# Alternating the high and low matmuls of the chunks with stationary weights in a float32 transformer block

## The chip, the cores and the metric

The kernel runs on one core of one Trainium2 chip, in one launch. The metric is the device time of the whole program in microseconds. Before the change it is 1725.64 us, the median of three runs (1724.52 to 1726.35).

## The reference

One layer of a hybrid streaming encoder, for 256 rows of 2048 columns, all in float32:

```
h = rmsnorm(x, g_mix);  z = h @ w_in            # 2048 x 14848
o_a = hgrn2_mixer(...)                           # gated linear recurrence, 16 heads
o_b = swa_sink_attention(...)                    # banded attention, 32 heads
x = x + concat(sigmoid(gate_a)*o_a, sigmoid(gate_b)*o_b) @ w_out      # 4096 x 2048
h = rmsnorm(x, g_mlp)
x = x + square(relu(h @ w_up)) @ w_down          # 2048 x 8192, 8192 x 2048
x = x + sigmoid(x @ w_ple_gate) * (p @ w_ple_proj)
return rmsnorm(x, g_final)
```

The change lies in `h @ w_up` alone, and there in seven eighths of its columns.

## The kernel before, in words

**Products in three parts.** Every large product is made of float32 operands that are split into a high part, rounded to the type that TensorE multiplies at one pass (`F32R` in the code), and a low part, the rounding's remainder. Of the four products of parts the kernel keeps three: high by high, low activations by high weights, and high activations by low weights. The activations lie transposed in SBUF as `hT` (128 partitions, 16 slices of the contraction, high or low, 2 row tiles, 128 rows); `hT_hi` and `hT_lo` are its halves.

**Chunks.** The weights stream through SBUF in 588 chunks of 256 rows by 512 columns (two slices `kk` of 128 rows). SyncE loads a chunk into one of 4 slots of `w_raw`. ScalarE rounds it into `w_hi` (`split_hi`, L980), once the slot's former user has been read (`w_used` of four chunks earlier). VectorE subtracts and writes `w_lo` (`split_lo`, L1337); that also frees the slot of `w_raw`. TensorE works the chunks in order; `w_hi_ready` and `w_lo_ready` count the chunks split, and the last matmul of a chunk raises `w_used`. ScalarE and VectorE run ahead of TensorE and do the work between the products (`steps`, `mlp_steps`) in between, in an order written out by hand, three chunks behind the splits (`LAG`).

**Two shapes of chunk.** In most chunks the activations are the stationary operand (128 by 128) and the weights move, 512 columns at a time: twelve matmuls a chunk, at L679 (high activations), L680 (low activations) and L685 (low weights). In the chunks of `up` with `j > 0` it is turned around (`turned_chunk`): the weights are stationary, 128 columns of them at a time (`ct` 0 to 3), and the activations move. With `w_hi` stationary all 512 columns of `hT` move, high and low, 2 row tiles (L693). With `w_lo` stationary the 256 columns of `hT_hi` move (L699), and are added to the first half of the same PSUM bank. The result comes out transposed, as `down` needs it. Each `ct` has its own bank (`turned_acc`): two banks named `acc` and two named `turn`. So a turned chunk is 8 matmuls of 512 columns and 8 of 256, each with its own weight load of 128 by 128.

**Order and loops.** The up and down products come in groups of 1024 hidden columns. Two blocks `up` (8 chunks each) are followed by the four blocks `down` of the group before (16 chunks in all). `up` with `j = 1` stands before the loop; a hardware loop of 3 rounds does two groups a round, and what is left of `down` follows it. That makes 14 turned blocks, and behind each pair of them a stretch of 16 `down` chunks: seven pairs, seven stretches.

**The wait.** Before its first matmul a chunk waits for `w_hi_ready` (in `chunk`, L669). A turned chunk then issues its 8 matmuls on `w_hi`, waits for `w_lo_ready`, and issues its 8 on `w_lo`. The first chunk of a block has further waits, for PSUM banks that must be empty (`free_before`).

Of the kernel before, what the change touches and what calls it, by code (L numbers as in the profile page):

```python
# [34 lines left out]
P = 128  # L35
TT = 2
# [97 lines left out]
def program(nc, x, p, positions, g_mix, w_in, lb_logits, hgrn_norm_g, sinks, w_out,  # L134
            g_mlp, w_up, w_down, w_ple_gate, w_ple_proj, g_final, out):
    with ExitStack() as ctx:
        def sb(name, shape, dt=F32):
            return ctx.enter_context(nc.sbuf_tensor(name, shape, dt))
# [3 lines left out]
        hT = sb("hT", [P, KT, 2, TT, P], F32R)  # L142
        hT_hi, hT_lo = hT[:, :, 0], hT[:, :, 1]
        w_raw = sb("w_raw", [P, RAW_SLOTS, 2, COLS])
        w_hi = sb("w_hi", [P, W_SLOTS, 2, COLS], F32R)
        w_lo = sb("w_lo", [P, W_SLOTS, 2, COLS], F32R)
# [182 lines left out]
        def count(value, r=0, per=0):  # L329

            return value + r * per
# [71 lines left out]
        def turned_acc(col, ct):  # L403

            return (acc[(UP_BANKS + col) % 2] if ct < 2 else T[2 * col:2 * col + 2])[ct % 2]
# [52 lines left out]
        def bank(name):  # L458
            return T[uses[name][0]]
# [183 lines left out]
        def _(pe):  # L643
# [9 lines left out]
            def chunk(slot, r=0):  # L653
# [16 lines left out]
                if turned(kind, j):  # L670
                    turned_chunk(n, col, c, s, first, last, r)
                    return
# [15 lines left out]

            def turned_chunk(n, col, c, s, first, last, r):

                for kk in range(2):
                    for ct in range(4):
                        pe.matmul(turned_acc(col, ct)[:], w_hi[:, s, kk, ct * P:(ct + 1) * P],  # L693
                                  hT[:, 2 * c + kk].rearrange("p a t c -> p (a t c)"),
                                  start=first and kk == 0, stop=False)
                pe.wait_ge(w_lo_ready, count(n + 1, r, LOOP_CHUNKS))
                for kk in range(2):
                    for ct in range(4):
                        mm = pe.matmul(turned_acc(col, ct)[:, 0:TT * P], w_lo[:, s, kk, ct * P:(ct + 1) * P],  # L699
                                       hT_hi[:, 2 * c + kk].rearrange("p t c -> p (t c)"), start=False,  # L700
                                       stop=last and kk == 1)
                mm.then_inc(w_used, 1)
# [225 lines left out]
            for slot in TAIL:  # L928
# [7 lines left out]
                if n == DOWN7:  # L936
                    pe.wait_ge(p_landed, 16)
                    for t in range(TT):
# [3 lines left out]
                        for k in range(2):  # L942
                            mm = pe.transpose(bank(name)[:, k * P:(k + 1) * P],
                                              pe_sb[:, t, k * P:(k + 1) * P], ident[:])
# [877 lines left out]
```

## Time and profile before

| what | value |
|---|---|
| median of three runs | 1725.64 us |
| span of the profiled execution, first to last instruction | 1722.8 us |
| TensorE matmuls busy | 1700.2 us, 99% of the span, 8685 instructions |
| TensorE weight loads busy | 1416.5 us, 82% |
| VectorE busy | 1105.8 us, 64% |
| ScalarE busy | 925.0 us, 54% |
| mean granted TensorE clock | 0.998 |

The profile gives the profiled execution its span and no other time of its own. The median of the runs lies 2.8 us above that span. "Busy" is the share of the span in which at least one instruction of the engine is recorded. Matmuls overlap in the records, so the duration of one says less than the distance from its start to the next one's start; below that distance is called a step. PE is TensorE's matmuls, PEld its weight loads, DVE VectorE, ACT ScalarE, and a q behind a name is the engine's sequencer.

### The profile page before, as it was taken

Reading aid. Unit: us, or ns where it says so; the run is one execution under the profiler, and the core shown is the slowest. Engines: PE = TensorE matmul, PEld = TensorE weight load, DVE = VectorE, ACT = ScalarE, POOL = GpSimd, SP = SyncE. Lnnn points to the kernel's source line nnn. Section 1 sums busy time; section 2 is a strip of 40 time slices with the busy share of each in tenths; the row PEclk is TensorE's granted clock in tenths of the full one; section 3 lists DMA queues with packets and bytes.
Section 4 is the critical chain, followed back from the end, with each engine's and each line's share of the span. In section 5 each row is a group of like instructions: output and inputs, shape, how many; then the busy total and the mean of one; then the engine's idle time right before and its main releaser. Section 6 shows DMA issues by size and latency. Waiting matters only on the chain.

```text
span 1722.8 us, 23521 instructions
## 1 busy us (share of the span) xinstructions
PE 1700.2 (99%) x8685; PEld 1416.5 (82%) x8685; DVE 1105.8 (64%) x1409; ACT 925.0 (54%) x1227; POOL 18.2 (1%) x72
## 2 busy tenths in 40 slices
PE   7999999999999999999999999999999999999997
PEld 6887887788887888878888888888888888888886
DVE  6667866875668756687585555656555556566565
ACT  6566646555566555655546554544444445454454
POOL 4000000000000000000000000000000000000000
PEclk9999999999999999999999999999999999999999
DMA  6665555556655566555556666666666666666554
GB/s 221 203 176 172 172 177 164 172 179 176 184 180 171 175 180 186 172 173 178 176 178 212 184 191 188 194 189 193 189 192 188 193 185 191 190 191 186 182 181 138
DMA packets 163293, 315.35 MB, mean 183 GB/s; under 512 B 10161, under 2 KB 10482, under 8 KB 163058
## 3 DMA queue, kind: packets, MB, share of 16 engines
q1 hardware_dynamic: 162016, 312.01, 59.8%
q10 hardware_dynamic: 1170, 1.87, 0.3%
q8 instruction: 73, 1.20, 0.3%
q14 instruction: 34, 0.28, 0.0%
HBM read 311.74 MB, written 2.10 MB: 182 GB/s over the span
## 4 chain that ended last, share of the span: by engine, by line
PE 96%; ACT 2%; DVE 1%; DMA 0%; issue 0%; SPq 0%; ACTq 0%; DVEq 0%
PE acc L679 21%; PE acc L680 21%; PE acc L685 21%; PE acc L693 6%; PE turn L693 6%; PE turn L685 3%; PE turn L680 3%; PE turn L679 3%; PE turn L699 3%; PE acc L699 3%; PE turn L721 2%; ACT w_hi L980 0%; PE turn L772 0%; ACT pr L1033 0%; PE turn L748 0%; PE turn L819 0%
## 5 line engine op out<-in xcount | busy, mean ns | idle before, releaser
L1337 DVE TENSOR_TENSOR w_lo<-w_raw,w_hi 128x1024 fp32r<-128x1024 f32 x588 | 720.0, 1224 | 564.5 <-ACT w_hi L980 561.6
L980 ACT ACTIVATE w_hi<-w_raw 128x1024 fp32r<-128x1024 f32 x588 | 622.7, 1059 | 709.9 <-PE acc L685 452.9
L679 PE MATMUL acc<-w_hi,hT 128*128 128x512 f32 x1104 | 436.0, 395 | 4.2 <-DVE hT L1377 4.2
L680 PE MATMUL acc<-w_hi,hT 128*128 128x512 f32 x1104 | 430.9, 390 | 0.0
L685 PE MATMUL acc<-w_lo,hT 128*128 128x512 f32 x1104 | 295.4, 389 | 0.0
L679 PEld LDWEIGHTS acc<-w_hi,hT 128*128 128x128 f32 x1104 | 207.9, 188 | 48.1 <-ACT w_hi L980 5.3
L685 PEld LDWEIGHTS acc<-w_lo,hT 128*128 128x128 f32 x1104 | 207.3, 188 | 43.5
L680 PEld LDWEIGHTS acc<-w_hi,hT 128*128 128x128 f32 x1104 | 208.0, 188 | 41.6
L679 PE MATMUL acc<-w_hi,mT_hi 128*128 128x512 f32 x416 | 164.5, 395 | 0.0
L680 PE MATMUL acc<-w_hi,mT_lo 128*128 128x512 f32 x416 | 162.3, 390 | 0.0
L693 PE MATMUL acc<-hT,w_hi 128*128 128x512 f32 x448 | 140.2, 394 | 0.6 <-issue 0.5
L693 PE MATMUL turn<-hT,w_hi 128*128 128x512 f32 x448 | 138.8, 391 | 0.0
L685 PE MATMUL acc<-w_lo,mT_hi 128*128 128x512 f32 x416 | 111.4, 390 | 0.0
L693 PEld LDWEIGHTS turn<-hT,w_hi 128*128 128x128 f32 x448 | 84.1, 188 | 19.2
L679 PEld LDWEIGHTS acc<-w_hi,mT_hi 128*128 128x128 f32 x416 | 78.1, 188 | 18.0 <-ACT w_hi L980 2.4
L685 PEld LDWEIGHTS acc<-w_lo,mT_hi 128*128 128x128 f32 x416 | 78.1, 188 | 16.5
L680 PEld LDWEIGHTS acc<-w_hi,mT_lo 128*128 128x128 f32 x416 | 78.2, 188 | 15.6
L699 PE MATMUL turn<-hT,w_lo 128*128 128x256 f32 x448 | 90.3, 283 | 0.0
L699 PE MATMUL acc<-hT,w_lo 128*128 128x256 f32 x448 | 89.5, 282 | 0.0
L693 PEld LDWEIGHTS acc<-hT,w_hi 128*128 128x128 f32 x448 | 77.3, 190 | 11.4 <-issue 1.5
L699 PEld LDWEIGHTS acc<-hT,w_lo 128*128 128x128 f32 x448 | 77.0, 190 | 8.7
L699 PEld LDWEIGHTS turn<-hT,w_lo 128*128 128x128 f32 x448 | 69.5, 191 | 0.0
(250 smaller groups left out, 1554.9 us busy)
## 6 DMA issues: line engine op xcount, KB each, us to landing
w_raw<-in_w_in_dram SPq DMA_DIRECT2D x232, 512.0 KB, 3.7
w_raw<-in_w_up_dram SPq DMA_DIRECT2D x128, 512.0 KB, 3.7
w_raw<-in_w_down_dram SPq DMA_DIRECT2D x128, 512.0 KB, 4.6
w_raw<-in_w_out_dram SPq DMA_DIRECT2D x64, 512.0 KB, 3.8
w_raw<-in_w_ple_gate_dram SPq DMA_DIRECT2D x32, 512.0 KB, 4.5
x_sb<-in_x_dram SPq DMA_DIRECT2D x8, 256.0 KB, 7.8
w_raw<-in_w_ple_proj_dram SPq DMA_DIRECT2D x4, 512.0 KB, 4.4
out_dram<-x_sb SPq DMA_DIRECT2D x6, 256.0 KB, 3.0
```

The costliest lines, as they stand in the source:

```text
L679: pe.matmul(a, hi[:, k, t, :], w_hi[:, s, kk, :], start=first and kk == 0, stop=False)
L680: pe.matmul(a, lo[:, k, t, :], w_hi[:, s, kk, :], start=False, stop=False)
L685: mm = pe.matmul(acc_of(kind, j, col, t)[:], hi[:, k, t, :], w_lo[:, s, kk, :], start=False, stop=last and kk == 1)
L693: pe.matmul(turned_acc(col, ct)[:], w_hi[:, s, kk, ct * P:(ct + 1) * P], hT[:, 2 * c + kk].rearrange("p a t c -> p (a t c)"), start=first ...
L699: mm = pe.matmul(turned_acc(col, ct)[:, 0:TT * P], w_lo[:, s, kk, ct * P:(ct + 1) * P], hT_hi[:, 2 * c + kk].rearrange("p t c -> p (t c)") ...
L721: mm = pe.transpose(bank(name)[:, i * P:(i + 1) * P], src(i), ident[:])
L980: act.activation(w_hi[:, n % W_SLOTS], w_raw[:, n % RAW_SLOTS], ACT.Copy)\
L1337: dve.tensor_tensor(w_lo[:, n % W_SLOTS], w_raw[:, n % RAW_SLOTS], w_hi[:, n % W_SLOTS].bitcast(F32), ALU.subtract).then_inc(w_lo_ready, 1)
```

## The change

In a turned chunk the eight matmuls on `w_hi` no longer come first and the eight on `w_lo` last. For each `kk` and `ct` the matmul of 512 columns on `w_hi` is issued, and right behind it the one of 256 columns on `w_lo`, into the same bank. The wait for `w_lo_ready` therefore stands ahead of the chunk's first matmul, beside the one for `w_hi_ready`. The number, shapes and operands of matmuls and weight loads stay the same, and so do all signals.

```diff
             def turned_chunk(n, col, c, s, first, last, r):
 
-                for kk in range(2):
-                    for ct in range(4):
-                        pe.matmul(turned_acc(col, ct)[:], w_hi[:, s, kk, ct * P:(ct + 1) * P],
-                                  hT[:, 2 * c + kk].rearrange("p a t c -> p (a t c)"),
-                                  start=first and kk == 0, stop=False)
                 pe.wait_ge(w_lo_ready, count(n + 1, r, LOOP_CHUNKS))
                 for kk in range(2):
                     for ct in range(4):
-                        mm = pe.matmul(turned_acc(col, ct)[:, 0:TT * P], w_lo[:, s, kk, ct * P:(ct + 1) * P],
+                        cs = slice(ct * P, (ct + 1) * P)
+                        pe.matmul(turned_acc(col, ct)[:], w_hi[:, s, kk, cs],
+                                  hT[:, 2 * c + kk].rearrange("p a t c -> p (a t c)"),
+                                  start=first and kk == 0, stop=False)
+                        mm = pe.matmul(turned_acc(col, ct)[:, 0:TT * P], w_lo[:, s, kk, cs],
                                        hT_hi[:, 2 * c + kk].rearrange("p t c -> p (t c)"), start=False,
                                        stop=last and kk == 1)
                 mm.then_inc(w_used, 1)
```

## Rows read from the trace of the kernel before

**Rows 1.** Page, parts 1 and 2: busy time, share, instructions; TensorE's clock in tenths.

```profile
PE 1700.2 (99%) x8685; PEld 1416.5 (82%) x8685; DVE 1105.8 (64%) x1409; ACT 925.0 (54%) x1227; POOL 18.2 (1%) x72
...
PEclk9999999999999999999999999999999999999999
```

**Rows 2.** Page, part 4: the chain that ended last, by engine.

```profile
PE 96%; ACT 2%; DVE 1%; DMA 0%; issue 0%; SPq 0%; ACTq 0%; DVEq 0%
```

**Rows 3.** Waits: who waited for whom, us in total, times, longest.

```profile
ACT w_hi L980 <- PE turn L699: 158.3, 104, 2.5
...
PEld acc L679 <- ACT w_hi L980: 7.8, 5, 4.5
```

**Rows 4.** Page, part 5: TensorE's groups in turned chunks; count, busy, mean ns.

```profile
L693 PE MATMUL acc<-hT,w_hi 128*128 128x512 f32 x448 | 140.2, 394 | 0.6 <-issue 0.5
L693 PE MATMUL turn<-hT,w_hi 128*128 128x512 f32 x448 | 138.8, 391 | 0.0
```

**Rows 5.** Timeline of PE, first two turned chunks: start us, us, instruction, count.

```profile
945.37 0.62 PE L693 MATMUL acc<-hT,w_hi 128*128 128x512 f32 x2
...
947.19 0.40 PE L699 MATMUL acc<-hT,w_lo 128*128 128x256 f32 x2
947.42 0.40 PE L699 MATMUL turn<-hT,w_lo 128*128 128x256 f32 x2
...
947.90 0.40 PE L699 MATMUL turn<-hT,w_lo 128*128 128x256 f32 x2
948.14 0.63 PE L693 MATMUL acc<-hT,w_hi 128*128 128x512 f32 x2
948.61 0.62 PE L693 MATMUL turn<-hT,w_hi 128*128 128x512 f32 x2
...
949.98 0.40 PE L699 MATMUL acc<-hT,w_lo 128*128 128x256 f32 x2
...
950.93 0.63 PE L693 MATMUL acc<-hT,w_hi 128*128 128x512 f32 x2
```

**Rows 6.** Durations ns (min/median/max) of L699, 947.1 to 948.2 us.

```profile
L699 PE MATMUL acc<-hT,w_lo x4: 278/282/283, 947.2 to 947.8; 128*128 128x256 f32 x4
```

**Rows 7.** Timeline of PE L685, four matmuls a row, in two stretches of `down`.

```profile
1346.81 1.08 PE L685 MATMUL acc<-w_lo,aT_hi 128*128 128x512 f32 x4
...
1360.54 1.08 PE L685 MATMUL turn<-w_lo,aT_hi 128*128 128x512 f32 x4
1436.23 1.07 PE L685 MATMUL acc<-w_lo,mT_hi 128*128 128x512 f32 x4
...
1449.83 1.07 PE L685 MATMUL turn<-w_lo,mT_hi 128*128 128x512 f32 x4
```

**Rows 8.** Windows of L685 in `down` stretches: us, PE busy, PEld busy, clock, DMA.

```profile
996.90:1029.60 32.70, 12.97 (x48) 9.02 (x48) 1.00 0.63 196
1086.70:1119.40 32.70, 12.83 (x48) 9.07 (x49) 1.00 0.63 194
```

**Rows 9.** Timeline of all engines behind a turned chunk: matmuls and their next loads.

```profile
1079.55 0.40 PE L679 MATMUL acc<-w_hi,mT_hi 128*128 128x512 f32 x1
1079.55 0.19 PEld L680 LDWEIGHTS acc<-w_hi,mT_lo 128*128 128x128 f32 x1
1079.78 0.40 PE L680 MATMUL acc<-w_hi,mT_lo 128*128 128x512 f32 x1
```

**Rows 10.** Timelines of DVE, ACT and PE before the turned chunk of 1076.75 us.

```profile
1070.49 1.22 DVE L1337 TENSOR_TENSOR w_lo<-w_raw,w_hi 128x1024 fp32r<-128x1024 f32 x1 [0.26 <-ACT w_hi L980]
...
1071.42 1.06 ACT L980 ACTIVATE w_hi<-w_raw 128x1024 fp32r<-128x1024 f32 x1 [0.96 <-PE turn L699]
...
1076.75 0.63 PE L693 MATMUL acc<-hT,w_hi 128*128 128x512 f32 x2
```

**Rows 11.** TensorE's sequencer at L669: its separate waits, ns min/median/max.

```profile
L669 PEldq EVENT_SEMAPHORE x73: 51/51/2467, 57.0 to 1686.4; - x73
```

## The prediction

> **What bounds the kernel now.** I read the page's busy shares first, and there the reader sees TensorE's matmuls busy for 99% of the span at the upper of its two clock levels (nines in every slice, so 2.4 GHz) [rows 1]. Then the chain of waits: 96% of it is TensorE [rows 2]. Then the waits: TensorE hardly waits for the split weights (7.8 us in the whole run, all in chunks of the other shape), while ScalarE waits 104 times for the end of a turned chunk [rows 3]. So the splits run ahead, and only what shortens or lengthens TensorE's own steps can move the time. Last the timeline, for the length of a step, which is where this change acts.
>
> **How long a chunk takes.** L693 has 448 + 448 matmuls, eight a chunk, so 112 turned chunks [rows 4]. The second one runs from 948.14 to 950.93, which is 2.79 us: its eight steps of 512 columns take 949.98 - 948.14 = 1.84 us and its eight of 256 take 0.95 us [rows 5]. (Of another chunk the rows give 2.80, 1076.75 to 1079.55 [rows 9, 10]. I take 2.795.) Together the turned chunks are 112 x 2.795 = 313 us.
>
> Four kinds of step can be told apart:
> - 512 columns in a steady run of them: 13.60 us for 60 matmuls (1436.23 to 1449.83, five chunks of twelve), so 0.2267 us [rows 7].
> - 256 columns in a steady run: two in 0.24 us, so 0.120 [rows 5].
> - 256 columns right after a run of 512: the first two take 0.23 us together [rows 5], and the shortest duration of the eight is 278 ns where the usual is 283 [rows 6]. The first is thus some 5 to 7 ns short, about 0.113.
> - 512 columns right after the run of 256: two in 0.47 us (948.14 to 948.61), so 0.235 each, where the first turned chunk, which came from a run of 512, takes (947.19 - 945.37) / 8 = 0.2275 on average [rows 5]. The whole excess is 1.84 - 1.82 = 0.02 us a chunk.
>
> The first two steps differ by 0.2267 - 0.120 = 0.1067 us for 256 columns, 0.417 ns a column, one column at 2.4 GHz. Take the columns off either and the same 13.3 ns remain (0.2267 - 0.2133; 0.120 - 0.1067). So both steady runs cost columns plus a fixed 13.3 ns for each pair of load and matmul, whatever the length. I take that as the law, and two things as disturbances of a change between runs: 7 ns saved once, some 27 ns paid afterwards.
>
> **The change part by part.**
>
> *The order.* Nothing is added or removed: 8 long and 8 short steps a chunk before and after. By the law a pair is 0.2267 + 0.120 = 0.3467 us and the chunk 8 x 0.3467 = 2.773, against 2.795 now. That is 0.022 us a chunk, 112 x 0.022 = 2.4 us less. The trace shows no single short step between long ones. Its bounds by the nearest rows: a pair of at least 0.2267 + 0.113 = 0.340, if every short step is like the first of its run; at most 0.235 + 0.120 = 0.355, if every long step is like those right behind a run of 256. I take the law, since it fits both steady runs without a free constant, and an alternation that repeats is a steady run too; it lies between the bounds.
>
> *The weight load.* A load starts with the matmul ahead of its own (the load for L680 at 1079.55, with the matmul of L679, and L680's own at 1079.78) [rows 9]. So one load is in flight beside one matmul, and no order of matmuls lets loads run further ahead. Under a short matmul now lies the load of a long one's weights. It is the same 128 by 128, and short steps follow each other at 0.120 with it. No cost.
>
> *The same bank twice in a row.* The short matmul now adds to the bank that the long one ahead of it writes. L679 and L680 do that in each chunk of the other shape, at a step of 0.23 (1079.55 to 1079.78) [rows 9], like all steps there. No cost.
>
> *The earlier wait.* `w_lo_ready` is asked for at the chunk's start and no longer 1.84 us into it. Queued behind it are all matmuls of the chunk, and behind their end ScalarE's next split. For the chunk at 1076.75 the split is long done. ScalarE's split at 1071.42 was released by the end of a turned chunk, the fourth ahead of its own. That one ended 2 x 2.79 us before 1076.75, so the split is for the chunk after the one at 1076.75, and the latter's `w_lo` is the one from 1070.49, ended at 1071.71 [rows 10]. That leaves 5.0 us of cover. It is at the end of a pair of blocks, behind the extra work on activations, where the cover should be thinnest. Cost nothing; if the cover were gone, the wait would expose up to 1.84 us a chunk. The instruction itself is one more on the sequencer, 51 ns each [rows 11]. The 73 such waits that L669 already has leave no trace in the chain, where issue has 0% [rows 2], so I count nothing. If none were hidden it would be 112 x 0.051 = 5.7 us.
>
> *What is left behind.* In the `down` stretches behind the turned pairs steps come in two steady patterns. From 1346.81 to 1360.54 they are 13.73 / 60 = 0.2288, from 1436.23 to 1449.83 0.2267, for the same shapes [rows 7]. Of the seven stretches four show the first kind (12.97 us for 48 matmuls of L685) and three the second (12.83), of each kind one is shown [rows 8]. The slow kind costs 27 ns a chunk, 4 x 16 x 0.027 = 1.7 us over the run. Which kind a stretch takes seems to hang on how it is entered, and the change alters that for all seven. All fast would save 1.7 us, all slow cost 3 x 16 x 0.027 = 1.3 us. I can't tell which, and take zero.
>
> *The sum* is 1722.8 - 2.4 = 1720.4 us of span. The median lies 2.8 us over the span before, so 1723.2 us. A difference of 0.2% (3.45 us) is about what a measurement of this kernel can tell from none.
>
> **The rivals.**
> - *The short step is free of the extra.* Every short matmul behind a long one steps at 0.113, as the first of a run does in the trace. A pair is 0.340, a chunk 2.72, 112 x 0.075 = 8.4 us less: 1717.2 us. For it: the first short step is short in [rows 5, 6]. Against it: what that one saves is followed by long steps that pay more than it, so it may be lent and not given. Chance 0.20.
> - *The long step never settles.* Behind a short step each long one costs 0.235, and the short ones stay at 0.120. A pair is 0.355, a chunk 2.84, 112 x 0.045 = 5.0 us more: 1730.6 us, slower. For it: those are the two steps that the trace shows at that very change [rows 5], and now there are eight such changes a chunk instead of one. Against it: they come behind eight short matmuls, where loads had followed each other closely; one short matmul may leave no such trail. It decides from a pair of 0.3494 on (2.795 / 8), above which the order loses. Chance 0.16.
> - *The order doesn't matter.* Steps neither gain nor lose, or settle into a pattern like the slow one of `down` (0.2288 + 0.120 = 0.3488, a chunk of 2.79): 1725.1 to 1725.6 us. Chance 0.14. The Trainium skill (TensorE: Matmul & The Clock Gate, Step-by-step: what each phase is for) comes to the same by another road: it says that weights are read through a port of their own and that loading the next ones takes nothing from the running matmul. By it both orders would be exactly equal, and the time 1725.6. The constant 13.3 ns in both kinds of step [rows 5, 7] doesn't decide whether it is the load's doing; that the runs of short steps disturb the long ones behind them speaks against full independence.
> - *The earlier wait is exposed.* VectorE's split comes late for some chunks. With 5.0 us of cover [rows 10] it would take a delay of two chunks. If the first chunk of each of the 14 blocks lost 1.84 us it would be 25.8 us more, 1751 us. Chance 0.02. The wait's instruction unhidden (+5.7 us, 1728.9 with the forecast's gain) gets 0.02.
>
> **How the numbers follow.** The forecast has 0.46: 1723.2 us, its own range 1721.3 to 1724.8 with what the `down` stretches may add. Of it 0.06 lies beyond 0.2% faster (if those stretches also turn fast, 4.1 us less in all). Faster: 0.20 + 0.06 = 0.26, and I say 0.28, as some pairs may lie between 0.340 and 0.347. Slower: 0.16 + 0.02 + 0.02 = 0.20. The same: 0.52. The range reaches down over the free short step (1717.0) and up to 1729.5, which leaves out the full price of the step that never settles and the exposed wait.
>
> **What would show it.** In the timeline of a turned chunk the rows alternate L693 and L699; the distance from one L693 to the next is the pair: 0.347 by the forecast, 0.340, 0.355 and 0.349 by the rivals. The chunk is 2.77, 2.72, 2.84 or 2.79. The first short step of a pair sits 0.227 behind its long one. The waits list no wait of L693 for `w_lo`; if it does, the cover was misread. The windows of L685 in the seven `down` stretches show 12.97 or 12.83 us, and the difference to the four and three of before is to be booked apart from the change itself. The prediction is wrong if a pair lies outside 0.343 to 0.351, or if the time moves by more than 3.45 us.

## The result, and the profile after

The changed kernel takes 1728.11 us (median of 20 runs, 1725.96 to 1729.89), against 1724.89 us for the kernel before in the same runs (1724.05 to 1726.35). The ratio is 1.0017, 95% interval 1.0012 to 1.0023: 3.2 us slower, where 2.4 us less were forecast. The interval lies clear of 1, though the difference is only 0.2%. The profiled execution took 1728.99 us, 1.7 us more than its span.

From the page after, the span, the busy shares, the chain by engine, and the two groups of the turned chunks on `acc` (line, engine, operation, count, busy us, mean ns, idle before):

```profile
span 1727.3 us, 23633 instructions
...
PE 1704.1 (99%) x8685; PEld 1415.9 (82%) x8685; DVE 1105.4 (64%) x1409; ACT 924.8 (54%) x1227; POOL 16.6 (1%) x72
...
PE 97%; ACT 1%; DVE 1%; DMA 0%; issue 0%; SPq 0%; ACTq 0%; DVEq 0%
...
L695 PE MATMUL acc<-hT,w_hi 128*128 128x512 f32 x448 | 168.3, 398 | 1.3 <-issue 1.3
...
L698 PE MATMUL acc<-hT,w_lo 128*128 128x256 f32 x448 | 125.8, 281 | 0.0
```

TensorE has as many matmuls as before and bounds the kernel as before [rows 1, 2]. The long matmuls are longer, 398 ns on average where 394 stood [rows 4]. No wait for `w_lo` is behind it. The only wait of a matmul in these chunks is this one (who waited for what: us in total, times, longest; "issue" is idle time in which the engine waited for nothing that the profile shows):

```profile
PE acc L695 <- issue: 1.3, 2, 0.8
```

The timeline tells more. First a chunk of the third turned block, the first of the loop (start us, us, instruction, count):

```profile
1038.24 0.40 PE L695 MATMUL acc<-hT,w_hi 128*128 128x512 f32 x1
1038.48 0.28 PE L698 MATMUL acc<-hT,w_lo 128*128 128x256 f32 x1
...
1039.30 0.40 PE L695 MATMUL turn<-hT,w_hi 128*128 128x512 f32 x1
...
1041.07 0.40 PE L695 MATMUL acc<-hT,w_hi 128*128 128x512 f32 x1
```

Then one of the second turned block:

```profile
969.29 0.39 PE L695 MATMUL acc<-hT,w_hi 128*128 128x512 f32 x1
969.52 0.28 PE L698 MATMUL acc<-hT,w_lo 128*128 128x256 f32 x1
...
970.33 0.39 PE L695 MATMUL turn<-hT,w_hi 128*128 128x512 f32 x1
...
972.07 0.39 PE L695 MATMUL acc<-hT,w_hi 128*128 128x512 f32 x1
```

Three pairs take 1.06 us in the first and 1.04 in the second; chunks take 2.83 and 2.78 (2.827 and 2.773 on average over a block, from the starts that the trace holds to the ns). So there are two steady paces. The fast one is the forecast's, 0.3467 us a pair: 230 + 117 ns. The slow one repeats after three pairs, 233 + 117, 241 + 120, 236 + 113 ns, 0.3533 on average. Which one a block runs in can be read from windows of 17 us over the L695 instructions (window, its length, PE busy, PEld busy, clock, DMA): the faster a block goes, the more of its weight loads fall in the window.

```profile
972.30:989.30 17.00, 17.00 (x50) 9.18 (x50) 1.00 0.62 182
1038.40:1055.40 17.00, 17.00 (x49) 9.02 (x48) 1.00 0.63 187
```

All twelve blocks of the loop show 9.02 to 9.05, the slow pattern; only the blocks before the loop turn fast, and they do so behind the eight transposes that stand after their third chunk:

```profile
954.55 1.03 PE L720 MATMUL turn<-ident,u_sb 128*128 128x128 f32 x8
...
956.47 0.39 PE L695 MATMUL turn<-hT,w_hi 128*128 128x512 f32 x1
...
956.81 0.39 PE L695 MATMUL acc<-hT,w_hi 128*128 128x512 f32 x1
```

The account: 12 chunks at 2.773 and 100 at about 2.827 are 315.9 us, where 112 at 2.793 were 312.8. That is 3.1 us of the 3.2 us by which the medians differ. Added up from the starts of the two traces, the turned chunks take 316.1 and 313.0 us.

The spans of the two profiled executions lie further apart than that, 1727.3 and 1722.8. Of these 4.5 us, 3.0 are in the turned chunks. Another 0.7 lies ahead of the first turned chunk, which starts at 946.08 where it started at 945.37 [rows 5], although the two kernels are the same up to there, and 0.8 lies between the turned blocks, outside the steps of `down`. In the other runs whose kernel is the same up to there, the first turned chunk starts anywhere from 944.9 to 947.4 us. So one span tells little at this size, and the steps inside the chunks tell more.

The `down` stretches did not change. Two rows 5 chunks apart of a stretch on aT, and two of one on mT:

```profile
998.81 1.07 PE L685 MATMUL acc<-w_lo,aT_hi 128*128 128x512 f32 x4
...
1012.54 1.07 PE L685 MATMUL turn<-w_lo,aT_hi 128*128 128x512 f32 x4
1261.15 1.07 PE L685 MATMUL acc<-w_lo,mT_hi 128*128 128x512 f32 x4
...
1274.75 1.07 PE L685 MATMUL turn<-w_lo,mT_hi 128*128 128x512 f32 x4
```

13.73 and 13.60 us again [rows 7], and again four stretches of the first kind and three of the second.

### The profile page after: what moved, and what is told of

Read it like the earlier page. It is cut to its first block, busy times and chain, and to the rows that moved or that the text cites. A ratio compares the mean times of both kernels' runs of the same rounds, so it can differ in the third digit from the quotient of the medians.

```text
span 1727.3 us, 23633 instructions
## 1 busy us (share of the span) xinstructions
PE 1704.1 (99%) x8685; PEld 1415.9 (82%) x8685; DVE 1105.4 (64%) x1409; ACT 924.8 (54%) x1227; POOL 16.6 (1%) x72
## 3 DMA queue, kind: packets, MB, share of 16 engines
q10 hardware_dynamic: 1170, 1.87, 0.3%
## 4 chain that ended last, share of the span: by engine, by line
PE 97%; ACT 1%; DVE 1%; DMA 0%; issue 0%; SPq 0%; ACTq 0%; DVEq 0%
PE acc L679 22%; PE acc L680 21%; PE acc L685 21%; PE acc L695 6%; PE turn L695 6%; PE turn L679 3%; PE turn L685 3%; PE turn L680 3%; PE acc L698 3%; PE turn L698 3%; PE turn L720 2%; PE turn L747 0%; PE turn L771 0%; PE turn L818 0%; PE turn L759 0%; DMA w_raw<-in_w_in_dram 0%
## 5 line engine op out<-in xcount | busy, mean ns | idle before, releaser
L685 PE MATMUL acc<-w_lo,hT 128*128 128x512 f32 x1104 | 296.0, 390 | 0.0
L685 PEld LDWEIGHTS acc<-w_lo,hT 128*128 128x128 f32 x1104 | 207.8, 188 | 43.7
L695 PE MATMUL acc<-hT,w_hi 128*128 128x512 f32 x448 | 168.3, 398 | 1.3 <-issue 1.3
L695 PE MATMUL turn<-hT,w_hi 128*128 128x512 f32 x448 | 168.1, 398 | 0.0
L698 PE MATMUL acc<-hT,w_lo 128*128 128x256 f32 x448 | 125.8, 281 | 0.0
L698 PE MATMUL turn<-hT,w_lo 128*128 128x256 f32 x448 | 125.8, 281 | 0.0
L685 PE MATMUL acc<-w_lo,mT_hi 128*128 128x512 f32 x416 | 111.5, 390 | 0.0
L695 PEld LDWEIGHTS acc<-hT,w_hi 128*128 128x128 f32 x448 | 84.1, 188 | 22.6 <-issue 2.1
L695 PEld LDWEIGHTS turn<-hT,w_hi 128*128 128x128 f32 x448 | 84.1, 188 | 20.8
L685 PEld LDWEIGHTS acc<-w_lo,mT_hi 128*128 128x128 f32 x416 | 78.1, 188 | 16.6
L698 PEld LDWEIGHTS acc<-hT,w_lo 128*128 128x128 f32 x448 | 84.6, 189 | 0.2
L698 PEld LDWEIGHTS turn<-hT,w_lo 128*128 128x128 f32 x448 | 84.6, 189 | 0.0
```

The costliest lines, as they stand in the source:

```text
L685: mm = pe.matmul(acc_of(kind, j, col, t)[:], hi[:, k, t, :], w_lo[:, s, kk, :], start=False, stop=last and kk == 1)
L695: pe.matmul(turned_acc(col, ct)[:], w_hi[:, s, kk, cs], hT[:, 2 * c + kk].rearrange("p a t c -> p (a t c)"), start=first and kk == 0, stop ...
```

## The experiments

All change `turned_chunk` or the place of buffers. The diffs are cut to the lines that matter. Where the order changes, the rest is the changed kernel with its early wait; where only a buffer moves, the rest is the kernel before unless the text says otherwise. A run marked "one execution" was timed once: its steps, which repeat from chunk to chunk, are read, and its time is only given beside them. `grouped(g)` below stands for the order: g long matmuls, then their g short ones, until the chunk's eight pairs are done. `grouped(8)` is the order before, `grouped(1)` the changed one.

**The wait alone.** The order before, with the wait at the chunk's start.

```diff
+                pe.wait_ge(w_lo_ready, count(n + 1, r, LOOP_CHUNKS))
                 for kk in range(2):
                     for ct in range(4):
                         pe.matmul(turned_acc(col, ct)[:], w_hi[:, s, kk, ct * P:(ct + 1) * P],
 ...
-                pe.wait_ge(w_lo_ready, count(n + 1, r, LOOP_CHUNKS))
```

> The order of before (eight long matmuls, then eight short), with only the wait for the low part moved to the chunk's start. Theory (two steady patterns of the alternating stream, 0.3467 and 0.3533 us a pair, the second being the price): the wait costs nothing, a turned chunk stays at 2.79 us and the time is that of before. Rival (the earlier wait or its instruction costs): a chunk of 2.82 us and 3 us more than before.

Measured: 1725.40 us, ratio 1.0005 (0.9995 to 1.0014). A block of it runs from chunk to chunk as before:

```profile
1058.12 0.63 PE L695 MATMUL acc<-hT,w_hi 128*128 128x512 f32 x2
...
1063.71 0.63 PE L695 MATMUL acc<-hT,w_hi 128*128 128x512 f32 x2
```

Two chunks in 5.59 us, and all turned chunks together 313.0 us, as in the trace before. The earlier wait and its instruction cost nothing that the trace shows; the order carries the cost.

**Two by two.**

```diff
-                for kk in range(2):
-                    for ct in range(4):
+                for what, kk, ct in grouped(2):
```

> Two long matmuls, then their two short ones, four times a chunk, so that no matmul adds to the bank of the one ahead of it. Rival (writing one bank twice in a row costs 6.7 ns a pair): the cost is gone, the chunk is 2.77 us and the time some 2.4 us under before. Theory (steady patterns that depend on how a stretch is entered): again one or two steady patterns with a mean pair between 0.3467 and 0.3533, chunk 2.77 to 2.83, whatever the bank; 0.3467 is the floor.

Measured: 1724.71 us, ratio 1.0000 (0.9990 to 1.0009). The chunk is 2.787 us in one pattern throughout, here 1062.52 to 1065.31:

```profile
1062.52 0.63 PE L695 MATMUL acc<-hT,w_hi 128*128 128x512 f32 x2
...
1065.31 0.62 PE L695 MATMUL acc<-hT,w_hi 128*128 128x512 f32 x2
```

With the double write to one bank gone the chunk is still not 2.77, so the rival of the bank is not borne out, though this run changes the order too. The run with equal lengths below settles it, and so do the alternating blocks that run at 2.773 us with every bank written twice in a row.

**Four by four.**

```diff
-                for kk in range(2):
-                    for ct in range(4):
+                for what, kk, ct in grouped(4):
```

> Four long matmuls, then their four short ones, twice a chunk. Theory: chunk 2.77 to 2.83, no step pattern under 0.3467 a pair on average. Rival (each change from short to long costs a fixed sum, 20 ns a chunk for one change before): two changes cost 40 ns, chunk 2.81 us, and two-by-two would be 2.85 us.

Measured: 1727.03 us, ratio 1.0014 (1.0004 to 1.0023), chunk 2.807 us. By itself it would fit a fixed price per change of length, 14 ns for the second. But four changes (two by two) cost 6 ns less than one, and eight cost 34 more or 20 less. No fixed price per change fits.

**Other entries.** The first chunk of a block in another order, the rest alternating.

```diff
+                if c:
+                    return grouped(1)
+                if n < HEAD_CHUNKS:
+                    return grouped(8)
+                second = n - HEAD_CHUNKS >= LOOP_CHUNKS // 2
+                if second:
+                    return grouped(8) if col else grouped(4)[:8] + grouped(1)[8:]
+                return grouped(2) if col else grouped(8)
```

> Alternating as in the changed kernel, but the first chunk of a block is ordered otherwise: eight by eight in both blocks before the loop and in the first and last block of a loop round, two by two in the second, four by four for its first slice in the third. Theory: the chunks behind settle in 2.774 us (0.3467 a pair) or 2.827 us (0.3533), the same one in all three rounds for the same entry, and at least one of the entries reaches the fast pattern, as the burst of transposes in the first turned block did in the changed kernel. Rival (the slow pattern belongs to the loop's code, say to its register waits, and the fast one to the chunks before the loop): all chunks in the loop stay at 2.827 us whatever the entry.

Measured (one execution, 1727.40 us): the second block of each loop round, entered two by two, is fast in all three rounds (9.19 or 9.20 us in its window); the other three are slow. Eight by eight threw the second block before the loop out of the fast pattern that the first had ended in. Windows over L695 of that second block, and of the first two of a round:

```profile
972.10:989.10 17.00, 17.00 (x49) 9.02 (x48) 1.00 0.60 180
1038.70:1055.70 17.00, 17.00 (x49) 9.06 (x49) 1.00 0.65 187
1061.30:1078.30 17.00, 17.00 (x50) 9.20 (x50) 1.00 0.61 182
```

The entry changes the pace, and the loop's code can run either.

**More entries**, of the same kind.

```diff
+                if n < HEAD_CHUNKS:
+                    return grouped(2)
+                second = n - HEAD_CHUNKS >= LOOP_CHUNKS // 2
+                if second:
+                    return grouped(1) if col else grouped(3)[:6] + grouped(1)[6:]
+                return grouped(2) if col else grouped(2)[:4] + grouped(1)[4:]
```

> Alternating, with other entries: both blocks before the loop start with a chunk two by two; in a loop round the first block starts with one group of two by two and then alternates, the second with a whole chunk two by two, the third with two groups of three, the fourth as in the changed kernel. Theory: each entry leads to one of the two patterns, the same in all three rounds, and the fourth block goes on in the pattern of the third. Rival (chance, or drift within a block): the pattern differs between rounds or changes inside a block without a disturbance.

Measured (one execution, 1727.32 us): the same entry gave different paces. The first block of a round turned fast in round one and slow in the two others, where a loop jump lies ahead of it. The second, two by two, turned slow where it came from fast and fast where it came from slow. Yet the second block before the loop, also two by two, came from fast and stayed fast. The first two blocks of rounds one and two:

```profile
1038.10:1055.10 17.00, 17.00 (x50) 9.16 (x49) 1.00 0.63 187
1060.30:1077.30 17.00, 17.00 (x49) 9.02 (x48) 1.00 0.59 179
...
1216.30:1233.30 17.00, 17.00 (x49) 9.02 (x49) 1.00 0.63 186
1239.00:1256.00 17.00, 17.00 (x50) 9.19 (x49) 1.00 0.58 182
```

My expectation that an entry decides by itself failed. The starts to the ns show what was different: the fast pace has two patterns. One is 230 + 117 ns in every pair; the block that turned slow had come from it. The other is 233 + 117 and 231 + 113 in turn, with the same mean of 0.3467; the block that stayed fast had come from that one. So the pace goes with the entry together with the pattern that the stream comes in. Inside a block the pace never changed without a disturbance.

**Two by two at the entry of each pair of blocks.**

```diff
+                return grouped(2) if c == 0 and col == 0 else grouped(1)
```

> The changed kernel, but the first chunk of each of the seven pairs of blocks goes two by two (two long, their two short), all others alternate. Two by two led the second block of a loop round into the fast pattern three times of three. Theory (two steady patterns, chosen by the entry): all chunks behind the first take 2.773 us, the turned chunks 310.7 us in all, 2.3 us less than before and 5.3 less than the changed kernel, so about 1722.5 us. Rival (what counts is the state in which the block before ended, and two by two helps only behind the slow pattern): behind a down stretch the chunks stay at 2.827 us and the time is that of the changed kernel, 1728 us.

Measured: in the trace all chunks behind the entries are fast, with 9.19 or 9.20 us in 13 windows and the 14th holding the transposes, all in the pattern 233 + 117, 231 + 113 ns; the turned chunks sum to 310.9 us, and the span is 1721.6. The time without a profile is 1724.47 us, ratio 1.0000 (0.9991 to 1.0009), where 1722.5 was expected. The interval still holds 0.9991, that is 1.6 us less. The profiled execution, 1723.34 us, is the shortest of the eleven, which go up to 1726.88. Whether the unprofiled runs took the fast pattern everywhere can't be seen, so this run shows that the fast pace can be had in every block and leaves its worth open.

**Short matmuls of 384 columns.**

```diff
-                        mm = pe.matmul(turned_acc(col, ct)[:, 0:TT * P], w_lo[:, s, kk, cs],
-                                       hT_hi[:, 2 * c + kk].rearrange("p t c -> p (t c)"), start=False,
+                        mm = pe.matmul(turned_acc(col, ct)[:, 0:3 * P], w_lo[:, s, kk, cs],
+                                       hT[:, 2 * c + kk].rearrange("p a t c -> p (a t c)")[:, 0:3 * P],
```

> The changed kernel with short matmuls of 384 columns instead of 256 (they add a fourth product of parts for one row tile, so more is computed than wanted). Theory (a pair of load and matmul costs its columns plus 13.3 ns; the slow pattern arises because a load just fits into the short step): 0.2267 + 0.1733 = 0.400 us a pair in all blocks, a chunk of 3.20 us, and only one pattern. Rival (any change of length disturbs the steps): again two patterns, or steps of the long ones of 0.233 to 0.241, and a chunk of 3.25 us in the loop.

Measured (one execution, 1779.37 us): two paces again, 0.4133 us a pair (chunk 3.307) and 0.4067 (chunk 3.253), neither of them 0.400. From a slow block and from a fast one, eight pairs each:

```profile
1072.56 0.40 PE L695 MATMUL acc<-hT,w_hi 128*128 128x512 f32 x1
...
1075.86 0.40 PE L695 MATMUL acc<-hT,w_hi 128*128 128x512 f32 x1
1142.51 0.39 PE L695 MATMUL acc<-hT,w_hi 128*128 128x512 f32 x1
...
1145.76 0.39 PE L695 MATMUL acc<-hT,w_hi 128*128 128x512 f32 x1
```

Six of the fourteen blocks are fast and eight slow, and here the transposes in the first block end the fast pace instead of starting it. My explanation, that the load only just fits under a step of 256 columns, is wrong: with some 55 ns more room (a short step of 175 ns) the slow chunk lies 107 ns over the law's, where it lay 54 over. The law is not kept here even at the faster pace. No run has 384 columns alone, so its term for them, 0.1733, is itself untested.

**Both matmuls of 512 columns.**

```diff
-                        mm = pe.matmul(turned_acc(col, ct)[:, 0:TT * P], w_lo[:, s, kk, cs],
-                                       hT_hi[:, 2 * c + kk].rearrange("p t c -> p (t c)"), start=False,
+                        mm = pe.matmul(turned_acc(col, ct)[:], w_lo[:, s, kk, cs],
+                                       hT[:, 2 * c + kk].rearrange("p a t c -> p (a t c)"),
```

> The changed kernel with both matmuls of a pair 512 columns long (the second adds the product of the low parts, which is more than wanted). Theory now (it is the alternation of lengths that disturbs, not the alternation of w_hi and w_lo as loads and not the same bank twice): all steps 0.2267 us, a chunk of 3.627 us, in one pattern. Rival (same bank or alternating sources of the load): steps over 0.2267, a chunk of 3.68 us or more, or two patterns.

Measured (one execution, 1819.29 us): 227 ns a step, 3.627 us a chunk, in all blocks; here one of sixteen steps, 3.63 us:

```profile
1049.32 0.39 PE L695 MATMUL acc<-hT,w_hi 128*128 128x512 f32 x1
...
1052.95 0.39 PE L695 MATMUL acc<-hT,w_hi 128*128 128x512 f32 x1
```

Same bank twice, `w_hi` and `w_lo` loaded in turn, 16 loads a chunk: all free here. What costs is that the lengths change. This run has no short step, so it says nothing on a load under one.

**The address of aT.** Of the kernel before, with 64 bytes of padding ahead of `u_sb`.

```diff
+            lb_("pad", [P, 16])
             u_sb = lb_("u_sb", [P, 2, TT, COLS])
```

> The kernel of before with 64 bytes of padding a partition ahead of u_sb, so that aT_hi, aT_lo, pT_hi and pT_lo begin at a multiple of 128 bytes, as mT and hT do; nothing else. It is on the step of 0.2288 us in four down stretches (those whose stationary operand is aT). Theory: the address of the stationary operand sets it, and all seven stretches show 0.2267 (12.83 us in the windows), some 1.8 us less. Rival (the prediction's: how a stretch is entered decides): nothing changes, four stretches stay at 12.97 us.

Measured: 1723.29 us, ratio 0.9990 (0.9981 to 0.9999), 1.6 us less. All seven stretches are of the fast kind. A stretch on aT, five chunks:

```profile
1355.21 1.07 PE L686 MATMUL acc<-w_lo,aT_hi 128*128 128x512 f32 x4
...
1368.81 1.07 PE L686 MATMUL acc<-w_lo,aT_hi 128*128 128x512 f32 x4
```

13.60 us, where such a stretch took 13.73 [rows 7]. The four stretches save 0.4 us each in the trace, which is the 1.6 us. The address decides, and not the entry, as I had put it.

**The mirror.** The padding ahead of `mT_hi` instead.

```diff
+        sb("pad", [P, 16])
         mT_hi = sb("mT_hi", [P, 8, TT, P], F32R)
```

> The kernel of before with the 64 bytes of padding ahead of mT_hi instead, so that mT begins 64 bytes past a multiple of 128 and aT, behind it, at a multiple. Theory (a stationary operand 64 bytes off a multiple of 128 costs 2.3 ns a step): now the stretches on aT run at 0.2267 us and the three on mT at 0.2288, and so do the output projection's chunks on mT. Rival (something else of aT, or the padding's other effects): the four or none of them are slow.

Measured (one execution): 1731.02 us. Five chunks on aT take 13.60, five on mT 14.00:

```profile
1360.54 1.07 PE L686 MATMUL acc<-w_lo,aT_hi 128*128 128x512 f32 x4
...
1374.14 1.07 PE L686 MATMUL acc<-w_lo,aT_hi 128*128 128x512 f32 x4
1443.71 1.10 PE L686 MATMUL acc<-w_lo,mT_hi 128*128 128x512 f32 x4
...
1457.71 1.10 PE L686 MATMUL turn<-w_lo,mT_hi 128*128 128x512 f32 x4
```

The direction is as expected. The size is not: 0.2333 us a step, 6.7 ns over the fast one and not 2.3.

**The weights moved 64 bytes.** Order as before.

```diff
+        sb("pad", [P, 16])
         w_hi = sb("w_hi", [P, W_SLOTS, 2, COLS], F32R)
         w_lo = sb("w_lo", [P, W_SLOTS, 2, COLS], F32R)
+        sb("pad2", [P, 16])
```

> The kernel of before with w_hi and w_lo moved 64 bytes off a multiple of 128 (padding ahead of w_hi and behind w_lo; mT stays at a multiple, aT at 64 past one). In the turned chunks they are the stationary operand, in all others the moving one. Theory (the address of what is loaded counts, since the load's reading gets in the way of the running matmul's): the turned chunks take more than 2.793 us, and the down stretches on mT keep their 0.2267 us a step. Rival (any operand's address counts, the moving one's too): the down stretches on mT and the chunks on hT slow down as well, and the whole kernel by 10 us or more.

Measured (one execution): 1736.52 us, against 1725.16 for the kernel before beside it. The theory fails. Of the rival, the slower mT and hT and the 10 us or more come out, but not its rule that any operand off its place costs: aT and the turned chunks get faster. Five chunks on aT, four on mT, and five on hT:

```profile
1179.04 1.07 PE L687 MATMUL acc<-w_lo,aT_hi 128*128 128x512 f32 x4
...
1192.64 1.07 PE L687 MATMUL turn<-w_lo,aT_hi 128*128 128x512 f32 x4
1445.85 1.10 PE L687 MATMUL acc<-w_lo,mT_hi 128*128 128x512 f32 x4
...
1457.05 1.10 PE L687 MATMUL turn<-w_lo,mT_hi 128*128 128x512 f32 x4
421.32 1.08 PE L687 MATMUL acc<-w_lo,hT 128*128 128x512 f32 x4
...
435.06 1.08 PE L687 MATMUL acc<-w_lo,hT 128*128 128x512 f32 x4
```

aT, off by 64 bytes like the weights, is now fast (13.60 for five chunks); mT, moved by 128 bytes in all, and hT, not moved, are slow (11.20 for four, 13.74 for five). It is the distance between the loaded and the moving operand that counts. The turned chunks got faster, 2.773 us in nearly all, in the order of before:

```profile
1051.95 0.62 PE L695 MATMUL acc<-hT,w_hi 128*128 128x512 f32 x2
...
1053.82 0.39 PE L701 MATMUL acc<-hT,w_lo 128*128 128x256 f32 x2
...
1054.05 0.39 PE L701 MATMUL turn<-hT,w_lo 128*128 128x256 f32 x2
...
1054.73 0.62 PE L695 MATMUL acc<-hT,w_hi 128*128 128x512 f32 x2
```

But not their long steps: eight long ones take 1.87 us here and took 1.84 [rows 5], the eight short ones 0.91 and took 0.95. The last six short steps take 0.68 us, 113.3 ns each, where a run of them stepped at 120; the long ones end up between 231 and 236, 233.3 on average over two. The two sum to 346.7 ns, as 226.7 and 120 do at the old distance. The moved weights shift time from the short step to the long one, and the chunk gains because the change of length costs less.

**The alternation with the weights moved so.** The same two lines of padding in the changed kernel.

> The changed kernel (alternating) with w_hi and w_lo 64 bytes off a multiple of 128, as in the run before, so that in the turned chunks the loaded and the moving operand no longer have the same remainder by 128 bytes. In the order of before that took the turned chunk from 2.793 to 2.773 us. Theory (the extra over columns plus 13.3 ns comes from the addresses at which load and stream read at once): the slow pattern is gone and all turned chunks take 2.773 us whatever the entry. Rival (the alternation of lengths makes the slow pattern by itself, whatever the addresses): most blocks of the loop stay at 2.827 us.

Measured (one execution): 1741.02 us; one pattern, 235 + 118 ns, 2.827 us a chunk in every block, also behind the transposes:

```profile
1046.15 0.40 PE L697 MATMUL acc<-hT,w_hi 128*128 128x512 f32 x1
...
1048.98 0.40 PE L697 MATMUL acc<-hT,w_hi 128*128 128x512 f32 x1
```

The theory falls. At this distance grouping by eight gives 2.773 and alternating 2.827, whatever the entry. So the slow pace comes with the alternation at both distances tried, and the fast one was seen only where loaded and moving operand have the distance that they have in the changed kernel. The long step, 235 ns, is much like the 233.3 of the grouped order at this distance; the short one is 118 and not 113.

**The weights moved 128 bytes**, order as before.

```diff
+        sb("pad", [P, 32])
         w_hi = sb("w_hi", [P, W_SLOTS, 2, COLS], F32R)
```

> A control: the kernel of before with 128 bytes of padding ahead of w_hi, so that everything behind moves but no remainder by 128 changes. Theory (only the remainder by 128 bytes counts): the trace of before again, turned chunks of 2.793 us, down stretches on aT at 0.2288 and on mT at 0.2267 us a step. Rival (any move of the weights against the activations shifts the patterns): other values.

Measured (one execution): 1745.33 us, against 1723.98 beside it. The control fails and with it the remainder by 128. Five chunks on hT take 13.95 us:

```profile
420.18 1.09 PE L686 MATMUL acc<-w_lo,hT 128*128 128x512 f32 x4
...
434.13 1.09 PE L686 MATMUL acc<-w_lo,hT 128*128 128x512 f32 x4
```

In the `down` stretches on aT and mT, whose distance from the weights did not change, it left the steps at 0.229 and 0.227 us.

Sorted by the distance modulo 256 bytes (address of the loaded operand less that of the moving one, addresses from the compiled program), all runs agree. By 512 bytes the remainders 192 (aT before) and 448 (hT with w +64) gave the same step, and so did 0 and 256, which is why the remainder is taken by 256. Steps are the trace's means in us. In the middle column the weights move; turned chunks load w and move hT:

```
distance   step of 512 columns in a run             turned chunk, grouped(8) / grouped(1)
0          0.2267 (hT, mT before; aT with padding)   2.793 / 2.827 or 2.773
64         0.2333 (mT in the mirror and with w +64)  2.773 / 2.827
128        0.2325 (hT with w +128)                   2.799 and 2.821 in turn / not run
192        0.2289 (aT before; hT with w +64)         not run
```

**Entry and padding together.**

```diff
+            lb_("pad", [P, 16])
             u_sb = lb_("u_sb", [P, 2, TT, COLS])
 ...
+                return grouped(2) if c == 0 and col == 0 else grouped(1)
```

> The alternating order entered two by two, and the 64 bytes of padding that align aT. Theory: the down stretches run at 0.2267 us a step (1.7 us less than before), the chunks behind each entry at 2.773 us (2.1 us less in all), since both kinds of stretch ahead of a block are now alike: about 3.9 us under before, 1721 us. Rival (the pattern of the trace is not what the runs without a profile do, as the kernel entered two by two was only 0.5 us under before): 1.7 us under before, no more, as with the padding alone.

Measured: 1722.23 us against 1725.42 for the kernel before on the same chip, ratio 0.9983 (0.9974 to 0.9992), 3.2 us less. The whole interval lies below the kernel before. The trace has all `down` stretches and all turned chunks behind their entries fast, and a span of 1719.7 us. 1.6 us of the gain is the padding's by the run above. The rest, some 1.6 us of the expected 2.1, would be the alternation's, but the intervals of this run and of the padding alone overlap, so that part is not shown by the times.

## Why the prediction was wrong

**The step that failed is the law taken for the alternation**: "an alternation that repeats is a steady run too", so 0.3467 us a pair. It is one of two paces at which the stream settles, and TensorE took the other, 0.3533, in all twelve blocks of the loop. The term *The order* was to be -0.022 us a chunk, 2.4 us less, and is +0.027 on average, 3.0 us more. The deciding point, 0.3494 a pair, lies between the two. The rival that never settles had the right sign, and nearly the size (0.355 against 0.3533). It had the mechanism half: long steps of 233 to 241 ns, as behind a run of short ones, but short steps of 113 to 120 and not all of 120. That the size is so near is partly luck: the long steps average 236.7 where it had 235, the short ones 116.7 where it had 120. I had given it 0.16 because a single short matmul "may leave no such trail"; it does.

**The sign of it could have been seen in the rows.** The long steps behind the short run (0.235) were the only rows of before with that change of length in them [rows 5], and I overruled them with a rule fitted to two runs without a change. The rule was no law even for runs of one length. With the weights moved by 64 bytes such runs step at 233.3 and 113.3 ns, which is the columns plus 20 and plus 6.7 ns. The one constant of 13.3 ns for both belongs to the distance that these buffers happened to have.

**The same bank and the earlier wait** were costed at nothing, and that holds: the run with equal lengths writes each bank twice in a row at 227 ns a step, and with the wait alone the turned chunks sum to 313.0 us as before. The cover of 5.0 us [rows 10] was not used up: no wait for `w_lo` appears.

**The load under the short matmul** was costed at nothing too, and this is open. A load fits under each step of a run of short ones, at 120 ns and, with the weights moved, at 113. What it does where long and short steps alternate, no run separates from the change of length. The reading that a load starts with the matmul ahead of its own holds for all matmuls of 256 columns or more in all sixteen traces: none of their loads starts sooner.

**What is left behind** was booked at zero, and it is zero: the steps of the seven stretches sum to the same within 0.1 us. The reason given, how a stretch is entered, was wrong: the distance between two buffers decides it.

**The 2.8 us from span to median** were partly chance. Each execution lasts 1.7 us longer than its own span, and the profiled one of before was the shortest of three. The median of twenty, 1724.89 us, lies 2.1 over that span, so the forecast by the same sum would have been 1722.5.

**The rule of the Trainium skill** (TensorE: Matmul & The Clock Gate, Step-by-step: what each phase is for), that loading the next tile's weights takes no SBUF read bandwidth from the running matmul, is not borne out as a rule that makes loads free. Of the operands of these matmuls only the loaded buffer was moved, by 64 bytes, and the step changed from 0.2289 to 0.2267 us, or from 0.2267 to 0.2333. Load and matmul do get in each other's way somewhere. Where, and whether it is the reading, no run shows.

**Left open.** Why the stream has just these paces (346.7 and 353.3 ns a pair, 406.7 and 413.3 with 384 columns, 6.7 apart both times), and why a change of length costs anything. What picks the pace is known only so far that the entry and the pattern ahead of it both matter. How often the runs without a profile take the one or the other pace is open too; the changed kernel's times spread over 3.9 us, the other's over 2.3, which would fit blocks that don't always choose alike, but this was only argued.

## What to carry to other kernels

Keep matmuls of one length together where TensorE is the bound, unless a measurement says otherwise: here groups of two, four and eight took 2.787, 2.807 and 2.793 us a chunk, and strict alternation 2.827 at its slow pace. Its fast pace, 2.773, beat all three, but no block of the loop found it by itself. A sequence of alternating lengths must be measured over whole blocks, since its pace depends on what ran ahead of it. When a row shows a step at exactly the change that an edit multiplies, price the edit by that row and not by the steady rate on either side. And look at the distance of the buffers that TensorE loads from and streams from: of the four tried, equal remainders by 256 bytes gave the shortest steps in runs of 512 columns, for 64 bytes of padding. In runs of 256 columns 64 bytes apart was shorter, 113 against 120 ns, so each shape has to be looked at.

## What the runs showed of the hardware that was not expected

- A stream of loads and matmuls with alternating lengths has more than one steady pace for the same instructions at the same clock level (0.3467 and 0.3533 us a pair for 512 and 256 columns, the faster one in two patterns of steps), and in all blocks traced it stayed in one until something disturbed it.
- The step of a 512-column matmul depends on the distance between the loaded and the moving buffer: 226.7, 228.9, 233.3 and 232.5 ns at 0, 192, 64 and 128 bytes modulo 256. The weights moved by 128 bytes gave 1745.33 us beside 1723.98. Of the 588 chunks 276 stand on hT; at 5.8 ns for each of their twelve matmuls that is 19.2 us, an estimate, and the turned chunks add 2.0 in the trace.
- A step of 256 columns answers the other way round: in runs of them 120 ns at 0 and 113.3 at 64 bytes, where 512 columns go from 226.7 to 233.3. The sum of the two stays 346.7.
- Two orders of the same matmuls answer to that distance in opposite ways: at 64 bytes the grouped chunk falls from 2.793 to 2.773 us, while the alternating one loses its fast pace.
